# Token sums of squares taken from the turned copy of the input, and first loads in another order, in a two-block transformer kernel

## The reference, cut to what matters

```python
def rms_norm(x, g):
    xf = x.astype(jnp.float32)
    y = xf * lax.rsqrt(jnp.mean(xf * xf, axis=-1, keepdims=True) + EPS)
    return (y * g.astype(jnp.float32)).astype(x.dtype)

# first_block, l = 0
h = rms_norm(x, attn_norm_g[l])
proj = h @ w_in[l]
...
x = x + merged @ w_out[l]
```

## Time and profile before

| | |
|---|---|
| median of 3 runs | 1470.04 us (1469.83 to 1470.35) |
| the profiled execution, its own time | 1469.65 us |
| its span in the trace | 1467.9 us |
| PE busy | 1459.9 us, 99% of the span |
| DVE, ACT, POOL busy | 1098.2, 884.2, 56.9 us |
| HBM read | 254.25 MB, 174 GB/s over the span |

### The profile page before, as it was taken

The page is one execution under the profiler, slowest core; times in us unless marked ns, Lnnn a source line. Parts: engine busy times, 40 slices in busy tenths (PEclk is TensorE's granted clock), DMA queues, the critical chain, the costliest instruction groups (busy, mean ns, idle before and its releaser), DMA issues.

```text
span 1467.9 us, 20026 instructions
## 1 busy us (share of the span) xinstructions
PE 1459.9 (99%) x7774; PEld 1235.0 (84%) x7774; DVE 1098.2 (75%) x1626; ACT 884.2 (60%) x1341; POOL 56.9 (4%) x69
## 2 busy tenths in 40 slices
PE   9999999999999999999999999999999999999998
PEld 7878888888898778888888888888888898888887
DVE  7897779996578878799956687875467567887446
ACT  6565657775447565677744586764456455766435
POOL 1110000000021000000000001000010000100001
PEclk9999999999999999999999999999999999999999
DMA  8643546666555435556665534656646543566562
GB/s 299 206 145 109 163 143 207 190 196 195 177 165 184 132 115 177 168 189 199 188 191 202 173 101 130 222 189 198 191 158 237 165 128 135 178 193 195 188 192 81
DMA packets 74015, 256.62 MB, mean 175 GB/s; under 512 B 8640, under 2 KB 9920, under 8 KB 73920
## 3 DMA queue, kind: packets, MB, share of 16 engines
q1 hardware_dynamic: 73776, 255.33, 54.5%
q10 hardware_dynamic: 144, 0.00, 0.0%
HBM read 254.25 MB, written 1.05 MB: 174 GB/s over the span
## 4 chain that ended last, share of the span: by engine, by line
PE 94%; DVE 3%; ACT 2%; DMA 0%; issue 0%; POOL 0%; SPq 0%; DVEq 0%; ACTq 0%; POOLq 0%
PE psum L1305 19%; PE psum L1332 18%; PE psum L1336 18%; PE psum L1334 18%; PE psum L1311 10%; PE psum L1261 4%; PE psum L1476 1%; PE psum L1508 1%; DVE w_low L2247 1%; ACT w_high L1727 1%; PE psum L1622 1%; PE psum L1569 1%; PE psum L1654 1%; PE psum L1325 1%; PE psum L1323 1%; PE psum L1326 1%
## 5 line engine op out<-in xcount | busy, mean ns | idle before, releaser
L2247 DVE TENSOR_TENSOR w_low<-w_raw,w_high 128x1024 fp32r<-128x1024 f32 (+2 forms) x482 | 574.2, 1198 | 209.0 <-ACT w_high L1727 207.8
L1727 ACT ACTIVATE w_high<-w_raw 128x1024 fp32r<-128x1024 f32 (+2 forms) x482 | 498.5, 1039 | 252.6 <-PE psum L1336 218.2
L1305 PE MATMUL psum<-x_parts,w_high 128*128 128x512 f32 x992 | 248.8, 393 | 0.0
L1305 PEld LDWEIGHTS psum<-x_parts,w_high 128*128 128x128 f32 x992 | 178.6, 189 | 32.1
L1332 PE MATMUL psum<-w_high,x_parts 128*128 128x512 f32 (+2 forms) x432 | 169.2, 392 | 1.0 <-DVE w_low L2247 1.0
L1336 PE MATMUL psum<-w_high,x_parts 128*128 128x512 f32 (+2 forms) x432 | 163.9, 379 | 0.0
L1334 PE MATMUL psum<-w_low,x_parts 128*128 128x512 f32 (+2 forms) x432 | 163.8, 379 | 0.0
L1311 PEld LDWEIGHTS psum<-x_parts,w_low 128*128 128x128 f32 x992 | 135.3, 190 | 9.7
L1311 PE MATMUL psum<-x_parts,w_low 128*128 128x256 f32 x992 | 138.3, 282 | 0.0
L1332 PE MATMUL psum<-w_high,ff_high 128*128 128x512 f32 x256 | 99.8, 390 | 0.0
L1334 PE MATMUL psum<-w_low,ff_high 128*128 128x512 f32 x256 | 99.6, 389 | 0.0
(11 more groups left out here) (296 smaller groups left out, 2322.2 us busy)
## 6 DMA issues: line engine op xcount, KB each, us to landing
w_raw<-in_weights SPq DMA_DIRECT2D x450, 512.0 KB, 3.7
w_raw<-in_weights SPq DMA_DIRECT2D x16, 384.0 KB, 3.1
w_raw<-in_weights SPq DMA_DIRECT2D x7, 416.0 KB, 3.7
rows<-in_second_rows SPq DMA_DIRECT2D x4, 512.0 KB, 4.9
w_raw<-in_weights SPq DMA_DIRECT2D x6, 256.0 KB, 2.7
scratch<-in_x_turned SPq DMA_DIRECT2D x4, 256.0 KB, 5.0
residual<-in_x SPq DMA_DIRECT2D x2, 512.0 KB, 7.0
dil_masks<-in_consts SPq DMA_DIRECT2D x1, 768.0 KB, 6.2
```

Source lines behind the costliest of these rows:

```text
L1305: eng.matmul(acc[:, f * PANEL:(f + 1) * PANEL], wh[:, j, f * P:(f + 1) * P], parts[:, k, :, :].rearrange("p s n -> p (s n)"), start=k == 0 ...
L1727: act(self.unit_view(self.wh, u), raw, ACT.Copy).then_inc(sem("w_high"), 1)
L2247: tt(self.unit_view(self.wl, u), raw, self.unit_view(self.wh, u), ALU.subtract).then_inc(sem("w_low"), 1)
```

## The change

Four edits.

1. The steps `square` of the first stage are gone. In their place a new step `tile_squares` squares `arriving` (features on partitions) on ACT in two instructions of 128 x 1024, into the second half of `scratch`, behind `split` 5.
2. Step `mean` of the first stage becomes three additions on POOL, of 128 x 512 each, which fold the 8 tiles to 2. A new step `token_sums` lets PE add up over the partitions: 4 products with the folded squares as weights and two columns of -0.5 as the moving operand. It stands behind unit 5, and `rstd`, `constants` and `diag` stand behind it. DVE's part of `rstd` scales the sums out of PSUM.
3. The DMAs of `x` leave loads 4 and 5 and become a step `load_x` behind the 28th unit; the residual sum waits for them.
4. SP waits for part 0 of x_turned to land before it issues part 2, and so load 3 and part 3 behind it.

```diff
@@ arrive
         self.after(2, later)
-        self.after(3, lambda: (add("square", g, 0), add("mean", g), self.prefetch(0, 6), add("square", g, 1),
-                               add("rstd", g)))
-        self.after(4, lambda: (add("constants"), add("diag", g)))
+        self.after(2, lambda: (self.prefetch(0, 5), add("tile_squares"), add("mean", g)))
+        self.after(3, lambda: self.prefetch(0, 6))
+        self.after(6, lambda: (add("token_sums"), add("rstd", g), add("constants"), add("diag", g)))
@@ build
         self.after(20, lambda: self.add("load_rest"))
+        self.after(28, lambda: self.add("load_x"))
@@ memory
+        self.tile_squares = [by_tile(self.scr[:, (2 + i) * UNIT:(3 + i) * UNIT]) for i in range(2)]
@@ sync
-                if 1 <= n <= 3:
-                    load_arriving(n)
-                elif 4 <= n <= 5:
-                    c = slice((n - 4) * PANEL, (n - 3) * PANEL)
-                    eng.dma_start(self.x[:, :, c], src[:, :, c]).then_inc(sem(f"x_loaded{n - 4}"), 16)
+                if n == 1:
+                    load_arriving(1)
+                elif n == 2:
+                    q.wait_ge(sem("x_arrived0"), 16)
+                    load_arriving(2)
+                elif n == 3:
+                    load_arriving(3)
...
+            elif kind == "load_x":
+                for half in range(2):
+                    c = slice(half * PANEL, (half + 1) * PANEL)
+                    eng.dma_start(self.x[:, :, c], src[:, :, c]).then_inc(sem("x_loaded"), 16)
@@ tensor
+            elif kind == "token_sums":
+                q.wait_ge(sem("pool_step"), 1)
+                q.wait_ge(sem("mean_ready"), at("mean", STAGE_MIX[0]))
+                for t in range(TT):
+                    for i in range(2):
+                        d = eng.matmul(bank[6][:, 2 * t:2 * t + 2], self.tile_squares[0][:, i, t * P:(t + 1) * P],
+                                       self.half[:, 0:2], start=i == 0, stop=i == 1, skip_group_check=True)
+                d.then_inc(sem("tokens_summed"), 1)
+                free[6] = (sem("mean_whole"), at("rstd", STAGE_MIX[0]))
@@ scalar
+            elif kind == "tile_squares":
+                for j in range(2):
+                    q.wait_ge(sem(f"x_arrived{2 * j + 1}"), 16)
+                    act(self.tile_squares[j], self.arriving[:, 4 * j:4 * j + 4, :], ACT.Square
+                        ).then_inc(sem("arrived_high"), 1)
@@ vector
+            elif kind == "rstd" and key[0] == STAGE_MIX[0]:
+                q.wait_ge(sem("tokens_summed"), 1)
+                sums = bank[6][:, 0:2 * TT].rearrange("p (t n) -> p t n", n=2)[:, :, 0]
+                ts(self.stat[:, 2:4], sums, -2.0 / D, EPS, ALU.mult, ALU.add).then_inc(sem("mean_whole"), 1)
...
+                if g == STAGE_FFN[0]:
+                    q.wait_ge(sem("x_loaded"), 32)
@@ gpsimd
+            if kind == "mean" and key[0] == STAGE_MIX[0]:
+                a, b = self.tile_squares
+                for n, part in enumerate((a, b)):
+                    q.wait_ge(sem("arrived_high"), DK + n + 1)
+                    q.step(tt(part[:, 0:2, :], part[:, 0:2, :], part[:, 2:4, :], ALU.add))
+                q.settle()
+                tt(a[:, 0:2, :], a[:, 0:2, :], b[:, 0:2, :], ALU.add).then_inc(sem("mean_ready"), 1)
```

More of the change, by code:

```diff
@@ L1061, in x_ready @@
     def x_ready(self, q, g, half):
-        if g == STAGE_MIX[0]:
-            q.wait_ge(self.sem(f"x_loaded{half}"), 16)
-        elif g in (1, 2, 3, 4):
+        if g in (1, 2, 3, 4):
             q.wait_ge(self.sem("x_added"), self.at("residual", g, half))
@@ L2831, in gpsimd @@
             kind, key = step[0], step[1:]
-            if kind == "mean":
+            if kind == "mean" and key[0] == STAGE_MIX[0]:
[5 more added lines that the diff above has]
+                tt(a[:, 0:2, :], a[:, 0:2, :], b[:, 0:2, :], ALU.add).then_inc(sem("mean_ready"), 1)
+            elif kind == "mean":
                 g, = key
```

## The result

The changed kernel takes 1474.39 us (median of 7 executions, 1473.60 to 1475.94) against 1470.04 before (7 executions, 1469.54 to 1470.35): a ratio of 1.0033, interval 1.0024 to 1.0043. It is slower by more than 0.2%, and 0.8 us outside the forecast range. The profiled execution took 1475.94 us with a span of 1474.1, against 1469.65 and 1467.9: 6.29 us more in its own time. It is the slowest of the seven, so what it shows is not yet the usual case.

The account below looks back on a forecast made before the run. PE, busy for 1459.9 of 1467.9 us, was taken to bound the kernel. Unit 4's -0.8, a wait of +1.7 and products of +0.88 made +1.8 us: 1471.8, within 0.2%, range 1469.9 to 1473.6.

Parts of the forecast that it names:

- unit 4 against 12.01: Start of unit 4 on PE: load 3 in a shorter DMA line brings it to 11.2, -0.8 us.
- one addition on POOL: Each 128x512 addition folding the squares on POOL takes 1.1 us, between bounds of 0.56 and 1.61.
- third addition ends: POOL's last addition stands behind DVE's subtraction for unit 6 until 16.4 and ends at 17.5.
- PE stands still: Ahead of the new products, PE is there at 15.84, the sums at 17.55: a wait of 1.7 us.
- products on PE: Four float32 products with two columns, ahead of unit 6, add 0.88 us to PE's path.
- unit 6 against 16.65: Unit 6's start on PE, where the shift is counted: +1.8 us, at 18.5.
- clock, us lost: PE's clock was expected to stay at 1.00 behind the pause; each 2 us at 1.2 GHz would add 1.
- rival 4: Load 3 still takes 6.5 us, unit 4 starts at 13.5, unit 6 +2.8 to +3.9: 1472.9 to 1474; chance 0.07.
- Rival 1: POOL's last addition runs beside or ahead of DVE, PE waits 0.5: +0.6, 1470.6 us; chance 0.26.
- rival 2: Ahead of unit 6, additions of 0.56 to 0.7 us leave no wait: about 0, 1470.0 us; chance 0.08.
- Rival 3: POOL's last addition loses to DVE twice and ends at 18.7, unit 6 at 19.7: +3.1, 1473.1 us; chance 0.12.
- the factor, `row` and `take_c` covered: Behind unit 6, the later factor was to hold up no PE work; at `row` it was covered by about 1 us.

Follow-up runs that it names:

- repeated run: The changed kernel measured once more with nothing altered: 1473.49 us (10 executions), ratio 1.0026; its profiled execution took 1473.45 us.
- filled pause: The changed kernel with seven products of 512 columns, results unused, ahead of PE's wait for POOL's last addition: 1472.56 us, ratio 1.0017.
- with ACT issuing: The kernel before with parts 1 to 3 of x_turned issued from ACT's queue instead of SP's: 1470.58 us, ratio 1.0006.
- longest pause: The kernel before with PE held ahead of unit 6 by a POOL power on 31 elements, no short products: 1475.90 us, ratio 1.0042.

## Why the prediction was wrong, step by step

| step | forecast | result's profile | repeated run's profile |
|---|---|---|---|
| unit 4 against 12.01 | -0.8 | +0.32 | -0.75 |
| one addition on POOL | 1.1 | 1.29 | 1.30 |
| third addition ends | 17.5 | 18.66 | 17.86 |
| PE stands still | 1.7 | 1.84 | 2.10 |
| products on PE | 0.88 | 1.26, part at half clock | 0.89 |
| unit 6 against 16.65 | +1.8 | +3.42 | +2.24 |
| clock, us lost | no term | 3.4 | 1.7 |

**What failed: the clock.** The last part of the prediction named a fall of the clock behind the longer pause as something that would make it wrong, and priced it (2 us at 1.2 GHz cost 1), but gave it neither a term nor a chance. Its ground was one row: the clock was 1.00 behind a pause of 1.02 us. That row says nothing of 1.7 to 2.1 us. Runs showed the fall in 15 of 17 executions of the changed kernel, at 1.7 us in the usual case and 3.4 in the profiled execution of the result and, by the mean clocks, in two more. It is most of the miss: of the 2.6 us by which the result's median lies above the forecast (+4.35 against +1.8) it is 1.7, and of the 1.9 us in the repeated run (+3.73) as much. The two executions without it are at +2.0 and +2.8 us; neither was profiled, so the rest of them is not split up. The cause, PE standing still, is shown by the filled pause. The Trainium skill (TensorE: Matmul & The Clock Gate, Part 1) says that the chip sets PE's clock by how busy PE has been recently, at half or full rate; the runs agree, with 0.50 and 1.00 as the only lasting levels.

**Unit 4's -0.8: not a gain of the edits.** The forecast took the 1.4 us by which load 3 starts later as more than returned by an emptier line. In the result's profile load 3 took 5.6 us instead of 6.5, a return of 0.9 against 1.2 lost. In the repeated run unit 4 was at 11.26. Over the profiles its start lies between 11.26 and 12.36 with SP's wait (eight kernels' profiles) and between 11.96 and 12.73 without it (eight; with ACT issuing, 12.94). The means are some 0.3 us apart, with one execution of each, and SP's wait alone gives a ratio of 1.0000: a gain of 0.8 is not there, a small one is neither shown nor excluded. The step took a landing that varies by up to 1.1 us from one execution to the next for a queue that can be emptied; rival 4's direction was right in the result's profile, its size (unit 4 at 13.5) was not.

**The additions and the third one's block: right in kind, short in size.** 1.29 us instead of 1.1 for each of the first two (the bounds were 0.56 and 1.61). The Trainium skill (GPSIMD Engine Reference, section 3.1) gives 4497 ns for 2048 elements; the quarter that I took as an estimate, 1.12 us, is short of the 1.29 measured here, and the measurement decides. DVE's turn came between the second and third additions, as forecast, and the third stood behind it: 16.53 to 18.66, which is 0.93 until the subtraction was over at 17.46 and 1.20 of its own.

**The exclusion works both ways, which the rows of before didn't show.** The subtraction of unit 6, 1.23 us alone, took 1.78, because it began while the second addition ran (until 16.45). The next one of DVE began at 17.46, while the third addition was still to run, and took 2.28 (until 15.76 + 3.98 = 19.74). Both subtractions together:

```profile
15.76 3.98 DVE L2269 TENSOR_TENSOR w_low<-w_raw,w_high 128x1024 fp32r<-128x1024 f32 x2 [1.76 <-ACT w_high L1743]
```

 The Trainium skill (SBUF — State Buffer, "Who interferes with whom") states it for either order; this trace agrees in both, within 0.2 us: 16.45 + 1.23 = 17.68 against 17.54, and 18.66 + 1.23 = 19.89 against 19.74. Here it cost PE only what it added to the third addition.

**The other rivals.** Rival 1 (the last addition beside or ahead of DVE) and rival 2 (no wait) didn't occur with POOL: PE waited 1.6 us or more in each profile that had all three additions there and nothing put in the place of the pause. Rival 2's condition, additions of 0.56 to 0.7 us and no wait, is met by the kernel with the additions on DVE: +0.39 us against its 0. Rival 2 had taken unit 4 0.8 us or more earlier for that, and in the profile unit 4 was 0.35 us later, so the near number is luck in part.

**Right as forecast.** The products' price without the clock (0.81 and 0.1 measured, 0.88 forecast); the two squares on ACT, 2.00 us for both, covered by units 4 and 5; the factor, `row` and `take_c` covered; x behind unit 28 at no cost; and nothing waiting later. Rival 3 (a second block of the last addition) didn't occur, although its time, 1473.1, is near the measured one: the right number would have come from the wrong mechanism. Its own sum is 0.1 too high, too: 16.4 + 1.23 + 1.1 + 0.88 is 19.6 for unit 6, +3.0. Of the 4.35 us of the medians, about 2 to 2.8 are the pause and the products with what unit 4's landing gave or took, and the rest is the clock. One reading was loose: the 1.02 us ahead of unit 4 is not the whole of PE's loss after its start, since the earlier trace rows has 0.5 us more at L1261, which the change left as it was.

**What stays open.** Which executions have the fall. The instruction stream is the same and the time of loads differs a little from one to the next, but the time of the landing was not varied by itself. Why the fall is twice as long in some (3 of 17 here, by the mean clock of 0.997 also 1 of 7 without SP's wait and 2 of 4 behind the longest pause) isn't settled either. Nor is why fewer executions fell with SP's wait or the late x taken back. No kernel of these beat the kernel before; the nearest were SP's wait alone (1.0000) and the additions on DVE (1.0003, interval 0.9994 to 1.0012).

## What to carry to other kernels

A pause of PE in the middle of dense work has two prices: its length, and, in part or all of the executions, slower work behind it; here, over all kernels with a pause of 1.6 to 2.1 us, it cost another 1.7 us or more in about 35 of 60 executions, and one row with a shorter pause and an unbroken clock was no evidence against it. Before an operation is given to POOL because POOL is idle, look at DVE's timeline in the same place: work on POOL there stood behind DVE's subtractions, while DVE itself had a free stretch of 1.8 us in which the same additions took 0.69 us each and no wait was left. And where single executions fall into two groups, compare the groups and count them; the difference of two medians then mixes what an edit costs with how many executions fell. The mean granted clock of each execution, where it is on record, tells the groups' cause without a profile of each.

## What the runs showed of the hardware that was not expected

- The clock can fall in one execution of a kernel and not in the next, behind the same pause: at 1.8 us in 6 of 10, at 2.45 us in 5 of 8. Each fall profiled but one cost 1.7 us, and that one 3.4.
- Sixteen passes of two columns in 1.70 us, without a pause, left the clock at 1.00 in the profile, and none of ten executions was in an upper group.
- A DVE subtraction stands behind a POOL addition (1.78 and 2.28 us instead of 1.23), as the addition does behind it (2.13 instead of 1.29).
- From 2 to 4 us the DMA engines moved 197 to 227 GB/s (202 before, 227 after, 197 with ACT issuing) and from 4 us on over 370 in the first two; a second issuing queue didn't raise the first figure.
